# Levels of the inverse in place, as a TensorE loop of five turns, with chain steps behind it

## The reference, cut to what matters

```python
def wkv_scan(r, decay, k, v, a_vec, b_vec, s0, reverse):
    def step(s, inp):
        r_t, w_t, k_t, v_t, a_t, b_t = inp
        sa = jnp.einsum('bhvk,bhk->bhv', s, a_t)
        s = s * w_t[:, :, None, :] + sa[..., None] * b_t[:, :, None, :] + v_t[..., None] * k_t[:, :, None, :]
        return s, jnp.einsum('bhvk,bhk->bhv', s, r_t)
...
for d in range(N_DIRS):
    reverse = d == 1
    yc_d, s_ctx = wkv_scan(r_c, dec_c, k_c, vh_c, -kk_c, kk_c * a_c, s0, reverse)
    yx_d, _ = wkv_scan(r_x, dec_x, k_x, vh_x, -kk_x, kk_x * a_x, s_ctx, reverse)
```

## Time and profile before

| | us |
|---|---|
| median of 3 runs | 4044.8 |
| lowest, highest run | 4040.22, 4048.21 |
| the profiled execution | 4041.35 |
| its span | 4039.5 |
| RWKV loop, 16 stages, in the span | 1151.3 to 1854.6 |
| PE busy in the whole span | 3755.7 (93%) |

### The profile page before, as it was taken

The page is one execution under the profiler, slowest core; times in us unless marked ns, Lnnn a source line. Parts: engine busy times, 40 slices in busy tenths (PEclk is TensorE's granted clock), DMA queues, the critical chain, the costliest instruction groups (busy, mean ns, idle before and its releaser), DMA issues.

```text
span 4039.5 us, 84245 instructions
## 1 busy us (share of the span) xinstructions
PE 3755.7 (93%) x35682; PEld 2377.6 (59%) x35682; DVE 1566.9 (39%) x3340; ACT 781.8 (19%) x1793; POOL 720.7 (18%) x621
## 2 busy tenths in 40 slices
PE   5999999999987877888999999999999999999998
PEld 4544444455556766665344444465788844658887
DVE  1412112154555555553322213552545334526353
ACT  2200000020144444442100002143000011520000
POOL 3200000000033334331000000001334400013343
PEclk8999999999999999999999999999999999999999
DMA  8289999962200000003499993110222211012221
GB/s 358 105 313 353 354 362 344 373 275 83 102 8 13 18 14 19 13 13 131 181 429 428 429 429 129 42 43 22 84 84 84 90 65 63 22 42 84 84 84 42
DMA packets 56387, 627.10 MB, mean 155 GB/s; under 512 B 5904, under 2 KB 9232, under 8 KB 20496
## 3 DMA queue, kind: packets, MB, share of 16 engines
q1 hardware_dynamic: 49664, 599.41, 37.4%
q0 software_dynamic: 3968, 14.16, 1.2%
q10 hardware_dynamic: 2448, 9.05, 0.6%
HBM read 604.50 MB, written 18.09 MB: 154 GB/s over the span
## 4 chain that ended last, share of the span: by engine, by line
PE 81%; DVE 7%; issue 5%; DMA 4%; ACT 2%; DVEq 1%; SPq 0%; ACTq 0%; PEld 0%; PEldq 0%
PE bank L947 65%; PE bank L1441 10%; DMA ring<-slabs 2%; DMA work<-slabs 2%; PE bank L1825 1%; PE bank L975 1%; PE bank L1833 1%; PE bank L1842 1%; DVE hx L2576 1%; PE bank L1497 1%; PE bank L1831 1%; DVE work L2552 0%; PE bank L1828 0%; DVE work L2913 0%; DVE resc L2799 0%
## 5 line engine op out<-in xcount | busy, mean ns | idle before, releaser
L947 PE MATMUL bank<-ring,work 128*32 128x256 f32 (+3 forms) x7002 | 763.3, 438 | 63.0 <-DMA ring<-slabs 54.9
L947 PE MATMUL bank<-work 128*128 128x256 f32 (+7 forms) x3478 | 717.0, 417 | 23.3 <-DVE work L2913 9.6
L947 PEld LDWEIGHTS bank<-work 128*128 128x128 f32 (+3 forms) x3478 | 463.9, 178 | 257.7 <-issue 196.9
L947 PEld LDWEIGHTS bank<-ring,work 128*32 128x32 f32 (+2 forms) x7002 | 316.5, 123 | 484.7 <-issue 389.3
L947 PE MATMUL bank<-hx,ring 128*128 128x512 f32 (+1 forms) x1344 | 484.3, 514 | 4.8 <-DVE hx L2576 2.8
L947 PE MATMUL bank<-work,ring 128*128 128x256 f32 (+1 forms) x1616 | 480.3, 455 | 6.2 <-DVE work L2862 3.1
L947 PEld LDWEIGHTS bank<-work,ring 128*128 128x128 f32 x1616 | 305.9, 190 | 174.2 <-issue 132.0
L947 PEld LDWEIGHTS bank<-hx,ring 128*128 128x128 f32 x1344 | 253.5, 190 | 223.4 <-issue 201.4
L3519 POOL TENSOR_TENSOR work<-ring 128x512 f32<-128x512 f32 (+1 forms) x44 | 69.3, 1575 | 1614.7 <-ACT work L2054 1217.6
L1441 PE MATMUL bank<-work 64*64 64x64 f32 x9216 | 228.8, 234 | 94.6 <-issue 75.6
L1441 PEld LDWEIGHTS bank<-work 64*64 64x64 f32 x9216 | 197.8, 144 | 116.4 <-issue 115.3
(11 more groups left out here) (353 smaller groups left out, 4688.1 us busy)
## 6 DMA issues: line engine op xcount, KB each, us to landing
ring<-slabs SPq DMA_DIRECT2D x228, 2048.0 KB, 10.1
work<-slabs SPq DMA_DIRECT2D x48, 2048.0 KB, 18.5
work<-kv SPq DMA_DIRECT2D x18, 384.0 KB, 3.0
kv<-work SPq DMA_DIRECT2D x2, 3072.0 KB, 15.7
kv<-work ACTq DMA_DIRECT2D x6, 512.0 KB, 17.6
work<-tabs ACTq DMA_DIRECT2D x1, 2176.0 KB, 8.2
resx<-xT SPq DMA_DIRECT2D x1, 2048.0 KB, 11.0
kv<-work POOLq DMA_DIRECT2D x1, 2048.0 KB, 7.0
```

Source lines behind the costliest of these rows:

```text
L947: return pe.matmul(out, lhsT, rhs, start=(k == 0), stop=(k == n - 1))
```

## The change

PE runs levels 0 to 4 in a loop of five turns with a register (`looped_levels`), the sixth behind it (`last_level`). For that every turn must do the same, so the levels work in place: `NT[d]` is overwritten by the HT copies and the one tile `TL` by the masked H; both directions share one `NT`. The four pairs of banks are fixed: group 0 has 0 to 3, group 1 has 4 to 7 (HT in 6 and 7 from column 192). PE signals a group once, after H and HT, and DVE's mask waits for that. DVE and ACT stay written out. The chain steps that stood in the levels now stand behind the loop: one after each half of the last level, then after the scores and the inverse products. The projections move to banks 4, 5, 7, 3, bonus to bank 4, kn 0 to bank 3. ACT takes the key factors before the third value copy and the four exponentials in three portions between levels; POOL's first batch waits for `e3` alone. "mean", "cen" and "sq" come after the third scores. Of PE's static instructions (a fp32 product counted once) 10763 are left of 13724; the other engines' counts do not change.

```diff
-LEVELS = 6
+LEVELS, LOOPED = 6, 5
...
+    RK_PE += [("kn", 0)] + _z() + [("kn", 1), ("var",)] if _d else []
+    RK_PE += [("L", _d, _l, _g) for _l in range(LOOPED) for _g in range(2)]
+    RK_PE += [("HT", _d, LOOPED, 0)] + _z() + [("HT", _d, LOOPED, 1)] + _z() + [("gate",), ("bonus",)] * _d
+    RK_PE += [("sb", _a, 0), ("sk", _a, 0)] + _z() + [("wu", _d, 0)] + _z() + [("wu", _d, 1)] + _z()
+    RK_PE += [("sb", _a, 1), ("sk", _a, 1)] + _z() + [("wu", _d, 2)] + [_n for _n in _zs]
+    RK_PE += [("ar", _d, 0), ("kv", _d, 0), ("sb", _a, 2), ("sk", _a, 2)] + [("mean",)] * _a + [("bc", _d, 0), ("ar", _d, 1), ("kv", _d, 1)]
...
+    RK_DVE += [("kkn",), ("yn",), ("ara", _a)] if _d else [("ksr",)]
+    RK_DVE += _z(2) + ([("res1",), ("lnx",), ("res",), ("bonus",)] if _d else [("ara", _a)]) + [("mt", _a, 0)] + _z() + [("kt", _a, 0)] + _z(2)
+    RK_DVE += [_n for _n in _zs] + [("mt", _a, 1), ("kt", _a, 1), ("yf", _a), ("ar", _d, 0), ("mt", _a, 2), ("kt", _a, 2)] + [("cen",)] * _a
...
-RK_BANK = {"vt": (0, 1), "x0": (2, 3, 2), "mv": (0, 1, 0), "kn": (1, 4), "var": (5,), "gate": (5,), "bonus": (6,),
+RK_BANK = {"vt": (0, 1), "x0": (2, 0, 2), "mv": (1, 0, 1), "kn": (3, 4), "var": (5,), "gate": (5,), "bonus": (4,),
...
-    elif _k in ("H", "HT"):
+    elif _k == "L":
+        RK_READ[_name] = {4 * _g + _b: [("lvd", ("T", _d, _l + 1, _g))] if _b < 2 else [("lva", ("HT", _d, _l + 1, _g))] for _b in range(4 - _g)}
+    elif _k == "HT":
+        RK_READ[_name] = {(2, 0)[_rest[2]] + _b: [("lvd", ("T", _rest[0], LEVELS, _rest[2]))] for _b in range(2)}
...
-        HTs, XT = (XX[:, 0, :, :], XX[:, 1, :, :]), XX[:, 1, :, :]
-        TL = [(NL, MT[d]) for d in range(2)]
+        XT, TL = XX[:, 0, :, :], NL
...
+            def looped_levels(p, d):
+                ts, hs = lv_count(LV_DVE, p, ("T", d, 0, 0)), lv_count(LV_ACT, p, ("HT", d, 1, 0))
+                for g in range(2):
+                    banks(p, "L", d, 0, g)
+                with pe.Fori(0, LOOPED) as i:
+                    for g in range(2):
+                        pe.wait_ge(lv_dve, i * 2 + (ts + g + 1))
+                        pe.wait_ge(lv_act, i * 2 + (hs - 2 + g))
+                        pe.sem_inc(pe_steps)
+                        level_products(level_banks("H", g), NT[d], TL, g)
+                        level_products(level_banks("HT", g), TL, NT[d], g).then_inc(rk_pe, 1)
...
+                    for l in range(1, LEVELS):
+                        level_copies(p, d, l)
+                        if l == 2 - d:
+                            inverse_decays(p, a)
+                        elif l == 3 - d:
+                            earlier_decays(p, a)
+                        elif l == 4 - d:
+                            own_decays(p, a)
+                        elif l == 4:
+                            variance_roots(p)
+                        elif l == 5 and d == 1:
+                            affine(p)
...
                     for l in range(1, LEVELS):
                         step_of(p, d, l, 0)
                         step_of(p, d, l, 1)
                         if l == 1 and d == 1:
                             normed_keys(p)
                         elif l == 4 and d == 1:
                             normed(p)
                             decayed_sums(p, a)
                         elif l == 4:
                             weighted_keys(p)
                         elif l == 5 and d == 1:
                             decayed_context(p, a)
                         elif l == 5:
                             decayed_sums(p, a)
```

More of the change, by code:

```diff
@@ L109 @@
[L109 to L116, removed]
@@ L1677, in _ @@
                     a = 1 - d
+                    steps = iter(range(1, NCH))
                     if d == 0:
@@ L3072, in _ @@
                     totals(p, d)
+                    steps = iter(range(1, NCH))
                     first_step(p, d, 0)
-                    chain(p, a, 1)
+                    chain(p, a, next(steps))
                     first_step(p, d, 1)
-                    chain(p, a, 2)
+                    chain(p, a, next(steps))
                     first_step(p, d, 2)
-                    for j in range(3, EARLY[d] + 1):
-                        chain(p, a, j)
+                    for _ in range(EARLY[d] - 2):
+                        chain(p, a, next(steps))
@@ L3080, in _ @@
                     scan(p, a)
-                    steps = iter(range(EARLY[d] + 1, NCH))
-                    for l in range(1, LEVELS + 1):
-                        step_of(p, d, l, 0) if l < LEVELS else inverse(p, d, 0)
-                        chain(p, a, next(steps))
-                        step_of(p, d, l, 1) if l < LEVELS else inverse(p, d, 1)
-                        if l == 2 and d == 1:
+                    for l in range(1, LEVELS):
+                        step_of(p, d, l, 0)
+                        step_of(p, d, l, 1)
+                        if l == 1 and d == 1:
@@ L3093, in _ @@
                             decayed_sums(p, a)
-                        elif l == LEVELS:
-                            decayed_context(p, a)
-                            if d == 1:
-                                with_bonus(p)
-                                v.tensor_copy(lnx, lnxn).then_inc(rk_dve, rk.one("lnx"))
-                    for j in steps:
-                        chain(p, a, j)
+                    for g in range(2):
+                        inverse(p, d, g)
+                        chain(p, a, next(steps))
@@ L3101, in _ @@
                     if d == 1:
+                        with_bonus(p)
+                        v.tensor_copy(lnx, lnxn).then_inc(rk_dve, rk.one("lnx"))
                         gated(p)
                         bonuses(p)
+                    else:
+                        decayed_context(p, a)
                     masked_scores(p, a, 0)
-                    masked_scores(p, a, 1)
+                    chain(p, a, next(steps))
+                    turned_keys(p, a, 0)
+                    for j in steps:
+                        if j < NCH - 1:
+                            chain(p, a, j)
```

181 lines of the change are left out of this document (94 added, 87 removed).

## The result

| | us |
|---|---|
| changed kernel, median of 6 runs | 4022.1 (4017.4 to 4025.9) |
| before, beside it, median of 6 runs | 4043.7 (4036.7 to 4049.3) |
| ratio, with its 95% interval | 0.995 (0.9939 to 0.9961) |
| second comparison (e5 below) | 0.9964 (0.9951 to 0.9976) |
| profiled execution after, its span | 4022.91, 4020.8 |

The change gains 16 to 22 us; the prediction said 66. The sign and the range held, the size did not: at most a third of it arrived. For the experiments the changed kernel's ratio is taken as 0.9957, the mean of its two comparisons; differences between two kernels have an uncertainty of some 8 us.

A forecast was written before the change was run, and what follows sets the result against it. PE's instruction fetch in the RWKV levels was taken as the bound. Gains less chain-step costs, 8 x (7.8 - 1.7) + 8 x (3.4 - 1.3), made 66 us: 3977 from a median of 4044.8; 3930 to 4025 holds 8 in 10.

The forecast's parts named there:

- The fetch: PE's levels run out of instructions; the loop takes q8 packets from 146 to about 98, "issue" from 99 to under 45 us.
- Rival 2: Loop's back edges restart fetch, 157 us less the 66: 4132; second form, "issue" is not fetch and stays: 4065; 9%.
- Chain steps behind the loop: Steps moved between scores and inverse products give back 1.7 us a stage in d = 0, 1.3 in d = 1.
- Key factors earlier: at nothing: Earlier key factors on ACT only let POOL begin sooner; no cost, save up to 1 us a stage if POOL is late.
- The scan's start: In d = 0 the fourth chain step, which starts DVE's scan, comes 0.7 us earlier.
- Turns of d = 0: Four turns after the first start at 1685.6, then every 1.9 us, plus 0.15 for an exponential, ending at 1692.5.
- The chain steps: Each moved step costs 0.2 us of PE; in d = 1 waiting behind masked scores adds about 0.5 us.
- The clock: PE's clock in the RWKV loop stays at 0.94 of full; slower turns at its lower level cost 7 us.
- code fetched ahead at the loop's exits: Each loop exit finds code already fetched, half a microsecond a stage, 8 us gained, cancelled against the clock's 7.
- d = 1's last turn: Before level 5's masks DVE does yn and the decayed sums, leaving PE idle 1.6 us.

The follow-up runs named there:

- e5: The changed kernel itself, unaltered, measured again beside the kernel before: 4023.3 us, ratio 0.9964 to before.
- e1: Changed kernel with the five turns of the levels written out in place of the loop: 4066.8 us, ratio 1.0071 to before.
- e12: e10 with the five turns of the levels written out in place of the loop: 4013.2 us, ratio 0.9934 to before.
- e3: Changed kernel with K-V products and mean exchanging banks 3 and 7: 4000.3 us, ratio 0.9905 to before.
- e2: Changed kernel with ACT's key factors back behind the first level's copies, in both directions: 4024.1 us, ratio 0.9969 to before.
- e9: Changed kernel with ACT's key factors behind the first level's copies in d = 0 alone: 4014.6 us, ratio 0.9945 to before.
- e7: Changed kernel leaving out the state update of chain steps behind the loop up to the tenth: 3988.7 us, ratio 0.9872 to before.
- e8: Kernel before the change with the same chain-step work left out as in e7: 4030.4 us, ratio 0.9975 to before.
- e6: Changed kernel with DVE's decayed sums earlier in the levels and weighted keys behind the first masked scores: 3991.1 us, ratio 0.9878 to before.
- e10: Changed kernel with the edits of e3, e4, e6 and e9 together: 3954.9 us, ratio 0.9796 to before.
- e11: e10 with DVE's normed keys moved ahead of the first masks of d = 1: 3950.4 us, ratio 0.9779 to before.
- e4: Changed kernel with gate product in bank 2 and bonus in bank 3, in place of 5 and 4: 4010.4 us, ratio 0.9939 to before.

## Why the prediction was wrong in size

- **The fetch: right.** Packets 146 to 97 (98 forecast), "issue" 29.7 us (under 45), the loop alone worth 46 us. Rival 2 is out, in both forms. The Trainium skill, "Runtime: NRT & Kernel Launch", section "Instruction fetch mechanics", calls the crossing of a block "mostly hidden". By that nothing was to be won; here a packet costs 0.94 us (e1) to 1.2 (e12: 56 us for 48 packets), so the trace disagrees.
- **The step that failed: where the last chain step now stands (16 to 21 us).** "Chain steps behind the loop" priced PE's time, bank 3 and the masks at 1.7 and 1.3 us a stage, and had no term for bank 7. It never asked who reads that bank last. Moved, the eleventh step's reader DVE L2954 holds the first K-V product 1.0 us in all 16 stages (e3). The mean's bank 3, which it did ask for at 0.7 us, costs 0.3.
- **"Key factors earlier: at nothing" (11 us by the loop, 5 by time).** The prediction asked what a late POOL costs, not what an early one collides with. It noted normed keys "slowed beside POOL" in d = 1 and did not carry that over to d = 0, where the subtraction stands ahead of the first masks (e2, e9).
- **The scan's start.** It was to come 0.7 us earlier; it starts 7.5 us into the stage as before. The first two chain additions of the stage come 0.4 and 0.6 us earlier, the third and fourth do not: PE makes the third step behind products that wait 0.39 us for DVE first. This was read, not tried.
- **Turns of d = 0 (1.4 us a stage, 11 in all).** A turn was right where nothing disturbs it (1.94 to 2.01, 1.9 forecast). But four turns of 1.9 and 0.15 make 7.75, where the prediction's times from 1685.6 to 1692.5 leave 6.9: a slip in the sum of 0.85. The four turns behind the late first masks took 8.3, the mean of eight stages. (The 0.25 us for semaphores and register values in a turn came from no row; the turns measured leave 0.3 for them.)
- **The chain steps: right or 6 us low in sum** (e7, e8), **but partly by luck.** The 0.5 us of wait behind the masked scores of d = 1 does not occur; waits of 0.6 in the last level, which the prediction did not name, stand in its place in both directions.
- **The clock: better than assumed.** The loop ran at 0.97 of full, before at 0.94, where the prediction took 7 us off for a clock that stays and cancelled them against 8 us for code fetched ahead at the loop's exits. No run shows that second term by itself; what is left of "issue" is 29.7 us.
- **d = 1's last turn: right in kind,** 1.74 us in place of 1.6, but its turns ended 2.0 us later than forecast, of which gate and bonus gave 1.6 back.

By stages: d = 0 was to shrink by 6.1 us and shrank by 1.6; its scores were to start at 20.9 and started at 24.3. d = 1 was to shrink by 2.1 and shrank by 0.7. For d = 0 the causes above fill the 4.5 us that are missing: 1.0 for bank 7, 1.4 for the subtraction, 0.7 for the scan, 1.4 for the turns; in d = 1, where 1.4 are missing, bank 7 is 1.0. Over all, 16 to 21, 5 to 11, 6 (the scan's start), 11 and up to 6 make 38 to 55 of the 44 to 50 us missing. Bank 7 and the subtraction were tried by runs; the scan's start and the turns are read from the timeline.

What stays open: why e6 and e3 gave more than the waits they took away (32 and 21 us for 18 and 16); the clock of the gate stretch explains some 5 and 3 us of it. The chain steps were not tried at other places.

## What to carry to other kernels

When a step moves, list every bank and buffer that it writes last, and ask who waits for that reader now; the wait falls on the next user of the bank, not on the step. When an operation is moved earlier, look at what it releases on GpSimd and which VectorE operation of the critical path it will then lie beside. The loop that stopped instruction fetch was worth its packets times about a microsecond, but only an order of the other engines made for it lets the rest of the gain through: here 16 to 22 us without, 82 with.

## What the runs showed of the hardware

- **VectorE and GpSimd block one another for whole instructions.** In d = 0 the scan keeps its 1.77 us, and POOL's product beside it goes from 1.81 to 3.39. The subtraction then stands until that product ends at 1585.50, and ends 0.83 us later. In d = 1, where the product starts at 1622.27 and so 1.0 us ahead of the scan, it keeps its 1.81, and the scan is the one that takes longer:

```profile
1623.31 2.41 DVE L2959 TENSOR_TENSOR_SCAN work<-tabs_sb,work 128x780 f32<-128x780 f32 x1
```

The Trainium skill, "SBUF — State Buffer", section "SBUF: two separate sides", says just that: the shared port pair is an exclusive lock, taken for a whole instruction by whichever comes first, a GpSimd operation or a VectorE one with two inputs in SBUF. Here the trace agrees (in d = 0 the two starts are 20 ns apart, too close to say which came first).
- **A back edge of a PE loop whose body is smaller than one packet costs no fetch:** over 64 back edges q8 brings 49 packets fewer than with the turns written out, and PE's idle between two turns is 0.23 us.
- **A longer wait can cost twice.** 0.3 us more of wait ahead of two 128x512 products (e2 against the changed kernel) went with a clock of 0.50 to 0.78 in 7 stages of 8 in place of 3, at up to 2.04 us each (5.01 against 2.97). Counted over all kernels with the PE loop, by the wait ahead of the last level in d = 1: with 0.8 us or less (e6, e10, e11) the stretch of gate and bonus was below full clock in 0 stages of 24; with 1.4 us in 1 of 5; with 1.7 to 1.8 us in 16 of 44; with 2.0 us (e2) in 7 of 7. But at the same 1.7 us it was 6 of 8 in e4 and 1 of 8 in e7, so the wait makes the low clock likelier and does not decide it. No run changed the wait alone.
